# Window-attention weights packed into one 128-column tile, and convolution steps moved into the gaps of a recurrence

## What is computed

```python
dist = q_idx + BLOCK - s_idx                 # a query block of 128 sees 256 keys: the block before and its own
mask = (dist >= 0) & (dist < WINDOW) & (key_pos >= 0)
s = where(mask, q @ k.T * 64**-0.5 - slope * dist, -inf)
m = maximum(max(s), sink)
p = exp(s - m); p = p / (sum(p) + exp(sink - m))
o = p @ v
```

## Time and profile before

| | us |
|---|---|
| three runs, median (lowest to highest) | 1091.87 (1090.0 to 1093.45) |
| the profiled execution, its own time | 1090.27 |
| its span from the first to the last instruction | 1088.5 |
| TensorE busy in the span | 1064.2 |
| VectorE busy | 688.7 |
| ScalarE busy | 532.7 |
| GpSimd busy | 115.9 |
| granted TensorE clock, mean, as a share of full speed | 0.999 |

### The profile page before, as it was taken

The page is one execution under the profiler, slowest core; times in us unless marked ns, Lnnn a source line. Parts: engine busy times, 40 slices in busy tenths (PEclk is TensorE's granted clock), DMA queues, the critical chain, the costliest instruction groups (busy, mean ns, idle before and its releaser), DMA issues.

```text
span 1088.5 us, 19513 instructions
## 1 busy us (share of the span) xinstructions
PE 1064.2 (98%) x7212; PEld 846.5 (78%) x7212; DVE 688.7 (63%) x2081; ACT 532.7 (49%) x1557; POOL 115.9 (11%) x152
## 2 busy tenths in 40 slices
PE   7999999999999999999999999999999999999997
PEld 5877787778778787777887878787787878787885
DVE  5285959584665747576365665757537575758565
ACT  4557675754636454363354535435344555564300
POOL 3413132134100000020000000002000000002210
PEclk9999999999999999999999999999999999999999
DMA  8967475665553626253562551715454343622432
GB/s 282 315 209 262 163 274 195 243 208 183 201 205 109 237 73 235 87 185 98 175 228 93 165 215 46 265 49 185 132 179 157 126 157 128 215 73 63 137 116 77
DMA packets 58430, 183.55 MB, mean 169 GB/s; under 512 B 8480, under 2 KB 21216, under 8 KB 45024
## 3 DMA queue, kind: packets, MB, share of 16 engines
q1 hardware_dynamic: 58192, 182.05, 48.7%
q10 hardware_dynamic: 144, 0.26, 0.1%
HBM read 138.22 MB, written 44.07 MB: 167 GB/s over the span
## 4 chain that ended last, share of the span: by engine, by line
PE 65%; DVE 6%; DMA 2%; issue 1%; ACT 0%; SPq 0%; DVEq 0%
PE bank L849 33%; PE bank L900 10%; PE bank L1137 4%; PE bank L957 2%; PE bank L990 2%; PE bank L972 2%; PE bank L1107 1%; PE bank L1120 1%; PE bank L1117 1%; PE bank L1121 1%; DVE y_cols L1797 1%; DVE y_step L1793 1%; PE bank L1030 1%; PE bank L1045 1%; PE bank L1115 1%
## 5 line engine op out<-in xcount | busy, mean ns | idle before, releaser
L849 PE MATMUL bank<-xr,w 128*128 128x512 f32 x2496 | 653.9, 405 | 7.4 <-DVE xr L1534 7.4
L849 PEld LDWEIGHTS bank<-xr,w 128*128 128x128 f32 x2496 | 449.8, 189 | 101.7 <-issue 9.8
L900 PE MATMUL bank<-wo,y_split 128*128 128x512 f32 x432 | 114.4, 404 | 0.0
L900 PEld LDWEIGHTS bank<-wo,y_split 128*128 128x128 f32 x432 | 77.0, 189 | 14.6 <-issue 0.7
L1582 DVE SCALAR_TENSOR_TENSOR kq<-conv_in,convw_all,kq 128x512 f32<-128x512 f32 x96 | 77.3, 806 | 7.8 <-ACT conv_in L1191 5.8
L1487 ACT ACTIVATE o_scaled<-bank 128x128 f32<-128x128 f32 x64 | 17.7, 277 | 124.5 <-PE bank L1121 124.3
L1353 ACT ACTIVATE score<-score,neg_max 128x256 f32<-128x256 f32 (+1 forms) x128 | 62.7, 493 | 29.0 <-DVE neg_max L1759 29.0
L1919 DVE TENSOR_SCALAR steps<-bank,nb_rk 128x128 f32<-128x128 f32 x64 | 22.3, 348 | 63.9 <-PE bank L1117 63.9
L1922 DVE SCALAR_TENSOR_TENSOR state<-state,cols_all,bank 128x128 f32<-128x128 f32 x64 | 22.2, 347 | 63.2 <-PE bank L1120 63.2
L1793 DVE TENSOR_TENSOR y_step<-blocks,y_cols 128x60 f32<-128x60 f32 (+14 forms) x240 | 50.3, 210 | 12.1 <-DMA blocks<-n_spill 3.3
L783 POOL TENSOR_TENSOR xr<-y_tile,xr 128x256 fp32r<-128x256 f32 x8 | 6.0, 774 | 455.1 <-ACT xr L1172 455.1
(11 more groups left out here) (217 smaller groups left out, 1628.3 us busy)
## 6 DMA issues: line engine op xcount, KB each, us to landing
w<-w_split SPq DMA_DIRECT2D x78, 1024.0 KB, 5.4
w_split<-w SPq DMA_DIRECT2D x26, 1024.0 KB, 5.1
blocks<-n_spill SPq DMA_DIRECT2D x32, 256.0 KB
y_spill<-y_out SPq DMA_DIRECT2D x30, 256.0 KB, 5.8
x_tile<-w_in SPq DMA_DIRECT2D x13, 512.0 KB, 6.1
y_tile<-w_in SPq DMA_DIRECT2D x12, 512.0 KB, 6.4
y_tile<-y_spill SPq DMA_DIRECT2D x12, 512.0 KB, 6.1
x_tile<-x SPq DMA_DIRECT2D x12, 512.0 KB, 3.9
```

What stands on the lines that cost most here:

```text
L849: ins = nc.tensor.matmul(bank[JOBS[at].bank][:], w[:, turn % 3, wp, k, :], xr[:, xp, k], start=(step == 0), stop=(step == 3 * KT - 1))
L900: ins = nc.tensor.matmul(bank[JOBS[at].bank][:], y_place(t)[:, yp, k], wo[:, k, wp, half * UNIT:(half + 1) * UNIT], start=(step == 0), sto ...
```

## The change

The weights of a row are brought from 256 columns to 128. Behind the row maximum VectorE takes the elementwise maximum of the two key blocks (a masked key holds a very low score), into the tile's own half, `band`. The exponentials are of 128 columns each, and one VectorE multiplication over 512 columns takes the place of the four scalings. TensorE transposes four tiles of a half in place of eight, all into bank 2. The product goes back through VectorE, not ScalarE: `part_band` multiplies the transposed tiles once by `past` (keys above the query's place) for the block before, and once by `tri` for the own block. It stands ahead of `base_inverses` for e = 0, and ahead of the recurrence for e = 1. The count of products in `values` stays as it was.

`convs` now counts single steps, nine for a slot. From slot 3 on there is no call ahead of `base_inverses`, at most the three steps of q are done ahead of the recurrence, and the rest goes one by one behind resid, v_new and state of the first two or three chunks (`conv_gap`); `slopes` moves behind the state of the third chunk. In slots 0 to 2 the calls stay where they were, each "one part" being one step now.

```diff
@@ -258,6 +258,7 @@
         closed = sb("closed", [P, P])
+        past = sb("past", [P, P])
         ones = sb("ones", [P, P])
@@ -362,6 +363,9 @@
         values_in = bank[5][:, 2 * P:4 * P]
+
+        band = score[:, :, :, P:2 * P]
+        earlier = score[:, :, :, 0:P]
@@ -483,8 +487,9 @@
         denom_step = counter("denom_step", 4)
-        p_scaled = counter("p_scaled", 8)
-        p_turn_done = counter("p_turn_done", 4)
+        packed = counter("packed", 2)
+        p_scaled = counter("p_scaled", 2)
+        p_turn_done = counter("p_turn_done", 2)
         p_turned_ready = counter("p_turned_ready", 4)
@@ -879,8 +884,6 @@
                 after(pe, g_ready, u, 1)
-                if u > 0:
-                    after(pe, p_turned_ready, JOBS[at].n, 4)
                 g = pre[:, 5].rearrange("p h t -> p (h t)")
@@ -959,19 +962,12 @@
             def turns(n, e):
-                s, i = divmod(n, AH)
-                if e == 1 and i == AH - 1 and s < SBS - 1:
-                    after(pe, ba_summed, s + 1, 1)
+                after(pe, p_scaled, n, e + 1)
                 for cc in range(2):
-                    after(pe, p_scaled, n, 4 * e + 2 * cc + 2)
-                    if cc == 0:
-                        after(pe, p_scaled, n, 4 * e + 4)
                     for hd in range(2):
-                        for kb in range(1 if (s, e, cc) == (0, 0, 0) else 2):
-                            q = 2 * hd + kb
-                            ins = nc.tensor.transpose(bank[2 + cc][:, q * P:(q + 1) * P],
-                                                      score[:, cc, hd, kb * P:(kb + 1) * P], ident[:])
-                    ins.then_inc(p_turn_done.sem, 1)
+                        q = 2 * cc + hd
+                        ins = nc.tensor.transpose(bank[2][:, q * P:(q + 1) * P], band[:, cc, hd], ident[:])
+                ins.then_inc(p_turn_done.sem, 1)
@@ -983,13 +979,13 @@
                     token = 4 * s + 2 * e + cc
-                    kbs = (0, 1) if token > 0 else (0,)
+                    kbs = (0, 1) if token > 0 else (1,)
                     for kb in kbs:
-                        key = (max(token - 1, 0) + kb) % 8
+                        key = (token - 1 + kb) % 8
                         for hd in range(2):
...
                                                    v_ring[:, key, hd * BD:(hd + 1) * BD], p_turned(cc)[:, 2 * hd + kb],
-                                                   start=(kb == 0), stop=(kb == kbs[-1]))
+                                                   start=(kb == kbs[0]), stop=(kb == kbs[-1]))
                 ins.then_inc(pv_done.sem, 1)
@@ -1345,27 +1341,17 @@
                 for cc in parts:
-                    keys = n_keys(n // AH, 2 * e + cc)
                     if cc == 0:
+                        after(act, packed, n, e + 1)
                         after(act, nmax_ready, n, e + 1)
                     for hd in range(2):
-                        sc = score[:, cc, hd, 0:keys]
+                        sc = band[:, cc, hd]
                         nc.scalar.activation(sc, sc, ACT.Exp, bias=neg_max[:, cc, hd:hd + 1],
...
                 nc.scalar.activation(sink_exp[:], sink_in[:], ACT.Exp).then_inc(sink_exp_ready.sem, 1)
-
-            def copy_turned(n, e):
-                for cc in range(2):
-                    after(act, p_turn_done, n, 2 * e + cc + 1)
-                    if n_keys(n // AH, 2 * e + cc) == P:
-                        pick = lambda a: a.rearrange("p (h k) n -> p h k n", k=2)[:, :, 0]
-                    else:
-                        pick = lambda a: a
-                    nc.scalar.activation(pick(p_turned(cc)), pick(tiles(bank[2 + cc])), ACT.Copy)\
-                        .then_inc(p_turned_ready.sem, 1)
@@ -1427,7 +1413,6 @@
                 after_jobs(n, 0.25)
-                copy_turned(n, 0)
                 after_jobs(n, 0.35)
@@ -1463,7 +1448,6 @@
                 after_jobs(n, min(at.p64, 0.66))
-                copy_turned(n, 1)
                 after_jobs(n, min(at.turns1, 0.66))
@@ -1547,6 +1531,7 @@
             nc.vector.tensor_scalar(closed[:], tri[:], -1.0, -MASKED, ALU.add, ALU.mult)
+            nc.vector.tensor_scalar(past[:], tri[:], -1.0, 1.0, ALU.mult, ALU.add)
             nc.vector.tensor_scalar(pair_all[:, :, NSINK], pair_all[:, :, SINK], -1.0, None, ALU.mult)
@@ -1568,21 +1553,20 @@
-            def conv(m, c, half):
+            def conv(m, c, step):
...
                 i = m % AH
-                if half == 0:
+                if step == 0:
                     after(dve, raw_copied, m, c + 1)
                     after(dve, tail_put, m, 1)
-                for step in (0,) if half == 0 else (1, 2):
-                    if step > 0:
-                        after(dve, conv_step, m, 2 * c + step)
-                    ins = nc.vector.scalar_tensor_tensor(acc, conv_in[:, c, step:step + UNIT],
-                                                         convw_all[:, i, c, step:step + 1], acc, ALU.mult, ALU.add)
-                    ins.then_inc(conv_step.sem if step < CONV - 2 else conv_ready.sem, 1)
-                if c == 2 and half == 1:
+                else:
+                    after(dve, conv_step, m, 2 * c + step)
+                ins = nc.vector.scalar_tensor_tensor(acc, conv_in[:, c, step:step + UNIT],
+                                                     convw_all[:, i, c, step:step + 1], acc, ALU.mult, ALU.add)
+                ins.then_inc(conv_step.sem if step < CONV - 2 else conv_ready.sem, 1)
+                if c == 2 and step == CONV - 2:
                     nc.vector.tensor_copy(tails[:, i], conv_in[:, :, UNIT:]).then_inc(tail_saved.sem, 1)
@@ -1697,16 +1681,21 @@
-            def convs(n, f, most=6):
-
-                while conv_place[0] < 6 * SLOTS and most > 0:
-                    m, part = divmod(conv_place[0], 6)
-                    c, half = divmod(part, 2)
+            def convs(n, f, most=9):
+
+                while conv_place[0] < 9 * SLOTS and most > 0:
+                    m, part = divmod(conv_place[0], 9)
+                    c, step = divmod(part, 3)
                     if JOBS[JOB_AT["qkv"[c], m]].end > n + f + 1e-6:
                         return
-                    conv(m, c, half)
+                    conv(m, c, step)
                     conv_place[0] += 1
                     most -= 1
+
+            def conv_gap(n, f):
+
+                if n >= AH - 1:
+                    convs(n, f, 1)
@@ -1749,7 +1738,7 @@
                     for hd in range(2):
-                        nc.vector.tensor_tensor_reduce(out=score[:, cc, hd, 0:keys],
+                        nc.vector.tensor_tensor_reduce(out=score[:, cc, hd, 2 * P - keys:],
                                                        in0=bank[2 + hd][:, cc * 256:cc * 256 + keys],
@@ -1758,6 +1747,8 @@
                     .then_inc(nmax_ready.sem, 1)
+                two = slice(1 if (s, e) == (0, 0) else 0, 2)
+                nc.vector.tensor_tensor(band[:, two], band[:, two], earlier[:, two], ALU.max).then_inc(packed.sem, 1)
                 after(dve, nmax_ready, n, e + 1)
@@ -1768,10 +1759,16 @@
                 after(dve, denom_step, n, 2 * e + 2)
-                for cc in range(2):
-                    for hd in range(2):
-                        p = score[:, cc, hd, 0:n_keys(n // AH, 2 * e + cc)]
-                        nc.vector.tensor_scalar(p, p, denom_inv[:, cc, hd:hd + 1], None, ALU.mult).then_inc(p_scaled.sem, 1)
+                nc.vector.tensor_tensor(band, band, denom_inv[:].unsqueeze(3).to_broadcast([P, 2, 2, P]), ALU.mult)\
+                    .then_inc(p_scaled.sem, 1)
+
+            def part_band(n, e):
+
+                after(dve, p_turn_done, n, e + 1)
+                turned = bank[2][:].rearrange("p (c h n) -> p c h n", c=2, h=2)
+                for half, keep in ((earlier, past), (band, tri)):
+                    kept = keep[:].unsqueeze(1).unsqueeze(1).to_broadcast([P, 2, 2, P])
+                    nc.vector.tensor_tensor(half, turned, kept, ALU.mult).then_inc(p_turned_ready.sem, 1)
@@ -1865,10 +1862,12 @@
                     weight_rest(n - 1, "bq")
-                convs(n, 0.2)
+                if n < AH - 1:
+                    convs(n, 0.2)
                 after_jobs(n, at.base)
...
                     split_y(9)
+                part_band(n, 0)
                 base_inverses(n)
@@ -1896,14 +1895,15 @@
                 divide(n, 1)
-                if n < SLOTS - 1:
+                if n < AH - 1:
                     slopes(n + 1)
...
                     split_y(11)
-                convs(n, at.p32)
+                convs(n, at.p32, 9 if n < AH - 1 else max(0, 9 * (n + 1) + 3 - conv_place[0]))
+                part_band(n, 1)
                 after_jobs(n, at.step0)
@@ -1915,17 +1915,26 @@
                     after_jobs(n, at.chunk(c, 1 / 3))
+                    conv_gap(n, at.p64 if c == 0 else at.chunk(c - 1))
                     after(dve, tr_done, n, c + 1)
...
```

(12 more changed lines are left out.)

## The result

The changed kernel takes 1107.2 us (median of four runs, 1103.1 to 1112.7) against 1091.1 us for the kernel before on the same chip: the ratio is 1.015, with an interval of 1.012 to 1.018. So it is slower by some 16 us, where 8 were forecast. The profiled execution of after is the longest of its four, 1112.7 us with a span of 1110.6; its rows hold some 5 us more than the median does.

A forecast was written before the change was run, and what follows sets the result against it. The prediction took TensorE, busy for 98% of the span, as the bound. New waits of 10.9 + 5.4 + 1.0 + 4.6 = 21.9 us against 13.8 saved made it 8.1 us longer, 1099 us, range 1087 to 1108.

The forecast's parts named there:

- The transposes: On TensorE, 120 transposes removed at 0.115 us each, priced from start to start, save 13.8 us.
- The rival at their duration of 0.25: Each removed TensorE transpose saves its whole duration, some 0.25 us: 30 us in all, time 1083; chance 0.02.
- The upper end of 2.2 for the two: Highest price for the two part_band instructions on VectorE, slowed where GpSimd is at work: 2.2 us, where 1.3 was taken.
- The first half: Ahead of the base inverses, VectorE's part_band makes TensorE wait at the first inversion product: 10.9 us in sum.
- 2.15 later: Slot 3, first half: the base inverses begin 2.15 us later; with the lost 0.2, 2.3 us.
- The second half: Ahead of the recurrence in slots 0 to 2, TensorE waits at `values` 1.8 us each, 5.4 us for three.
- free at 141.4: Slots 0 to 2, second half: VectorE is free at 141.4, not near 142.4, and the weights are ready at 142.8.
- The step in the residual's gap: Slots 4 to 6 and 8 to 10, second chunk: a convolution step makes L1120 late by 0.77 six times, 4.6 us.
- a forecast of 1.0: VectorE's packing ahead of L1884 adds 0.25 us of wait in slots 12 to 14, less in others: 1.0 us.
- The places hold: Rival at L1067: VectorE still finishes before TensorE arrives; 1077 with all waits absent, 1088 with only the first half's; chance 0.14.
- VectorE's slowed stretches shrink: Rival in slots 0 to 2: less slowing beside GpSimd takes away the second-half wait of 5.4, time 1093.6; chance 0.17.
- GpSimd in the way: Rival: part_band at its upper end of 2.2 adds 0.9 us in ten places, time 1108; chance 0.07.

The follow-up runs named there:

- experiment 1: The changed kernel with the convolution steps and bias left in their places of before, so the packed attention alone: 1137.4 us, ratio 1.041.
- experiment 3: The changed kernel without the convolution step in the gap that holds an output tile's residual (slots 4 to 6, 8 to 10): 1099.3 us, ratio 1.008.
- experiment 7: The changed kernel with slots 0 to 2 treated as the later ones, bias and steps in the recurrence's gaps: 1089.7 us, ratio 0.998.
- experiment 11: The kernel of experiment 8 with the first half of slots 3, 7, 11 and 15 in the old way (256 columns, ScalarE copies): 1079.8 us, ratio 0.989.
- experiment 10: The kernel of experiment 8 with each transpose done twice in 28 halves, 112 more transposes: 1095.4 us, 10.2 above experiment 8.
- experiment 12: The changed kernel with GpSimd's weight splitting cut from 1024 columns to 16 from the fourth weight tile on: 1094.8 us, ratio 1.002.
- experiment 4: The changed kernel with eleven idle TensorE products ahead of the second value products of slots 0 to 2: 1100.9 us, ratio 1.008.
- experiment 2: The kernel before with only the moved convolution steps and bias, without the packed attention: 1094.0 us, ratio 1.002.
- experiment 8: The changed kernel with the edits of experiment 7 and experiment 3 together: 1085.2 us, ratio 0.994.
- experiment 6: The kernel before with sixteen small ScalarE copies ahead of the last copy of the turned weights in slots 0 to 2: 1099.3 us, ratio 1.007.
- 5: The kernel before with nine small ScalarE copies ahead of the last copy of the turned weights in slots 0 to 2: 1093.6 us, ratio 1.001.
- 9: The kernel of experiment 8 with first-half parting, value products and second-half scores moved later in slots 3, 7, 11 and 15: 1092.6 us, ratio 1.001.

## Why the prediction was right and wrong

**Right: the sign and the places.** VectorE was the engine to watch, TensorE's new waits stand where the steps put them, and the single slots agree with experiments 1, 3, 7 and 11, each of which takes one away.

**The transposes.** Forecast 0.115 us each from starts; experiment 10 has 0.10 to 0.11 where nothing waits. The rival at their duration of 0.25 is out: it would have added 28 us there, and 10 were measured. The Trainium skill's 275 ns (TensorE: Matmul & The Clock Gate, "Part 4: PE-mode transpose") agrees with the mean duration of 273 ns in after, but it isn't the price of one among many.

**part_band.** Forecast 0.65 by starts; measured 0.68 each with a start 0.60 behind. The upper end of 2.2 for the two is out: the fourteen of 64 that run beside GpSimd's arithmetic last 0.68 like the others.

**The first half: 10.9 forecast, 7.4 measured, wrong in its parts.** By its steps the whole wait at L1063 would have been 3.8 and 10.9, 14.7; it is 11.2. Slots 7 and 11 have none and 1.2 where 1.9 each were due (in 7 TensorE had lost 3.2 to GpSimd shortly before), slot 12 has 2.0 for 1.5, slot 15 the 0.9 forecast. Slot 3 has 3.9 where 2.4 were due, and that is the failed step "2.15 later": it moved thirty instructions and kept their durations. They did begin 1.85 later. But they took 11.0 us in the earlier trace rows's slot and 12.5 in after, since more of them lie beside GpSimd's work (read from the timelines; experiment 11 shows that the wait comes with the parting, and none takes GpSimd away there):

```profile
240.10 0.21 DVE L1790 TENSOR_TENSOR y_step<-blocks,y_cols 128x60 f32<-128x60 f32 x1
...
240.34 0.65 DVE L1794 TENSOR_TENSOR y_cols<-y_step,ident 128x60 f32<-128x60 f32 x1
...
252.68 0.45 PE L1063 MATMUL bank<-steps,n_t 32*32 32x32 f32 x32 [3.93 <-DVE steps L1802]
```

Slots 0 to 2 have 1.1 each where 2.0 were due, by the same mechanism the other way round. The first two of the base inverses, 0.75 and 0.66 us beside GpSimd in slot 1 of before, are pushed clear of it by the parting, as slot 1 of after shows:

```profile
125.70 0.26 DVE L1790 TENSOR_TENSOR y_step<-blocks,y_cols 128x60 f32<-128x60 f32 x1
125.99 0.22 DVE L1794 TENSOR_TENSOR y_cols<-y_step,ident 128x60 f32<-128x60 f32 x1
```

**The second half: 1.8 forecast, 2.9 measured, three times.** The step that failed, "free at 141.4", kept the bias at its 0.60 us for two and took the scaling at 0.65, as if both stayed clear of GpSimd; GpSimd's four instructions, which ended at 138.7 in slot 1 of before, now lie over both. Experiment 12 takes GpSimd away and the wait is 1.6: with the durations of the forecast the sum is right to 0.2. That slots 0 to 2 as a whole would have been right but for the clock (2.4 us in experiment 4, 2.6 forecast) is luck: 1.1 too little here against 0.9 too much in the first half.

**The step in the residual's gap: 4.6 forecast, 4.3 measured** (six of 0.7 to 0.8). The waits of experiment 2 are the same, and experiment 8 has 4.5 by its time. At L1073 1.4 us stand for a forecast of 1.0: 0.2 each in slots 12 to 14, as forecast, and 0.8 in slot 4.

**The term that was missing: the clock.** I priced each wait by its length. Three of the forecast's waits came out at 2.9 and one at 3.9, and behind each TensorE ran at half clock for 3.4 to 6.8 us. Experiment 4 puts the price in slots 0 to 2 at 5.9 us, experiment 6 shows it with nothing of the change in the kernel, and slot 3 of after is 4.5 us longer, which is its 3.8 us of further wait less the 0.7 saved and some 1.4 more, about what 3.4 us at half clock cost. The same slot with the same wait of 3.9 bears that out: 71.5 us where 3.4 us are at half clock (after, 3, 4 and 7), 72.8 where 6.8 are (8 and 12). So the 8.1 us that the forecast lacks in slots 0 to 3 are 5.9 and 1.4 of clock, and 1.5 of wait in slot 3, less the 0.7 by which slots 0 to 2 without the clock stay under the forecast. In slots 0 to 2 it is GpSimd that makes the wait long enough: with it gone 1.6 us are left, and in the profiled execution no clock fell behind them.

**The rivals.** "The places hold" had its point right, 1.3 against margin plus relief: it holds in slots 4 to 6, 8 to 10, 13 and 14, and experiments 7 and 11 make it hold nearly everywhere, at 1079.8 us, near its 1077 (which keeps no wait, while 11 has given back 14 of the 120 transposes). "VectorE's slowed stretches shrink" failed: the second half's wait grew, because the slowing passed to the new scaling and the bias. "GpSimd in the way" gave 1108 and the time is 1107, but by another way, so its number is luck: the slowed instructions are the neighbours of part_band, not part_band.

## What to carry to other kernels

Price a new wait twice: its length, and the stretch at half clock that may follow it, from some 1.5 us on in these runs; there, where it came, the clock cost as much again as the wait, while 0.7 cost only itself. When an instruction of VectorE is moved or pushed back, lay GpSimd's timeline over its new place before keeping its duration. A change that trades TensorE's work for VectorE's is worth having only where VectorE has slack at the meeting point: the same edit was 16 us slower as it stood, and 12 us faster with room made in the first three slots, the residual's gap left free and the old way kept in the four halves that have no room.

## What the runs showed of the hardware

- The clock falls at shorter waits than I would have thought: behind 1.5 us (experiment 6), 1.75 (7, slot 12), 1.9 (8, slot 11), 2.0 (5, slot 11) and 1.9 to 2.9 (1), each time to 0.50 for 3.4 or 6.8 us. It did not fall behind 1.6 (12), 1.7 (8, slot 12), 2.0 (after, slot 12; experiment 11, slot 12), 2.4 (3, slot 11) and in 1 behind a 1.7, a 2.5 and a 2.2; and behind 1.0 to 1.4 only once, in 9, shortly behind another such stretch. By its mean clock the same kernel does it in some executions and not in others (6: 0.991 to 0.999). So length alone doesn't decide; what else does is open.
- Idle products in the wait (experiment 4) keep the clock up and are worth their place: a mean clock of 0.992 to 0.997 in ten executions against after's 0.986 to 0.991, and 6.3 us by the medians.
- GpSimd's arithmetic slows some of VectorE's instructions and not others: a scaling of two SBUF operands goes from 0.69 to 0.98 us, a bias of 256 columns with a scalar from 0.34 to 0.77 on average, a short dependent product from 0.21 to 0.65, while part_band, with one operand in PSUM, stays at 0.68. The Trainium skill (GPSIMD Engine Reference, "1. Specifications") states that its SBUF interfaces are shared with VectorE, with contention where VectorE has two SBUF inputs or runs in a two-port mode; these rows agree.
